# First block: the inner layer of the compressed keys and values with its operands exchanged, in four column tiles

## The reference

```python
def compress_blocks(tok, tok_idx, pos_emb, w1, w2):
    b, _, g, dh = tok.shape
    blk = tok[:, tok_idx] + pos_emb[None, None, :, None, :]
    flat = blk.transpose(0, 1, 3, 2, 4).reshape(b, tok_idx.shape[0], g, CMP_LEN * dh)
    return jax.nn.gelu(flat @ w1) @ w2
```

## Time and profile before

| | |
|---|---|
| three runs | 1532.93, 1535.36, 1536.45 us; median 1535.36 us |
| profiled execution, from its first to its last instruction | 1526.7 us (its time as a run is not given apart) |
| busy: TensorE / VectorE / ScalarE / GpSimd | 1497.1 / 1085.7 / 782.3 / 59.4 us |
| TensorE's granted clock | 9 tenths or more of full speed in all forty slices |
| DMA | 296.54 MB, mean 194 GB/s |

### The profile page before, as it was taken

How to read it: one execution, slowest core, us unless ns; L and a number is a source line. 1 busy time by engine, 2 the same in 40 slices (tenths; PEclk the granted TensorE clock), 3 DMA queues, 4 the chain that set the end, 5 groups by cost and what they waited for, 6 DMA issues and landing times.

```text
span 1526.7 us, 29330 instructions
## 1 busy us (share of the span) xinstructions
PE 1497.1 (98%) x12160; PEld 1457.3 (95%) x12160; DVE 1085.7 (71%) x1927; ACT 782.3 (51%) x1366; POOL 59.4 (4%) x61
## 2 busy tenths in 40 slices
PE   9999999999999999999999999999999999999999
PEld 8888899999898899999999989999999999999999
DVE  8777788887768778888984477665468646766653
ACT  6554586534644567633545545544444554454442
POOL 0000000000000000000030040000002102100000
PEclk9999999999999999999999999999999999999999
DMA  8124379997324269998343434545534444355552
GB/s 321 66 111 167 120 265 310 334 355 300 111 111 146 104 216 335 347 347 327 139 164 142 166 138 153 207 173 187 194 124 156 180 149 166 138 178 182 194 180 70
DMA packets 42435, 296.54 MB, mean 194 GB/s; under 512 B 5056, under 2 KB 5312, under 8 KB 6848
## 3 DMA queue, kind: packets, MB, share of 16 engines
q1 hardware_dynamic: 41888, 294.66, 52.7%
q10 hardware_dynamic: 416, 0.02, 0.0%
HBM read 293.61 MB, written 1.05 MB: 193 GB/s over the span
## 4 chain that ended last, share of the span: by engine, by line
PE 79%; DVE 10%; DMA 4%; ACT 3%; issue 2%; POOL 1%; SPq 0%; DVEq 0%; ACTq 0%
PE acc L766 23%; PE acc L767 23%; PE acc L768 23%; DMA ring<-stream 4%; DVE wL L1686 4%; ACT wH L1340 2%; PE ps_t L893 1%; PE acc L966 1%; PE acc L862 1%; PE ps_s L880 1%; PE ps_o L903 1%; PE ps_o L902 1%; PE ps_s L878 1%; PE acc L951 1%; PE acc L978 1%
## 5 line engine op out<-in xcount | busy, mean ns | idle before, releaser
L1686 DVE TENSOR_TENSOR wL<-ring,wH 128x1024 fp32r<-128x1024 f32 x444 | 548.6, 1243 | 274.6 <-ACT wH L1340 269.4
L766 PE MATMUL acc<-hH,wH 128*128 128x256 f32 x2208 | 638.4, 289 | 7.7 <-DVE wL L1686 3.5
L768 PE MATMUL acc<-hH,wL 128*128 128x256 f32 x2208 | 625.2, 283 | 0.0
L767 PE MATMUL acc<-hL,wH 128*128 128x256 f32 x2208 | 625.2, 283 | 0.0
L1340 ACT ACTIVATE wH<-ring 128x1024 fp32r<-128x1024 f32 x444 | 462.2, 1050 | 224.2 <-PE acc L768 117.5
L766 PEld LDWEIGHTS acc<-hH,wH 128*128 128x128 f32 x2208 | 423.8, 192 | 15.5 <-issue 9.6
L767 PEld LDWEIGHTS acc<-hL,wH 128*128 128x128 f32 x2208 | 424.0, 192 | 3.3 <-issue 2.6
L768 PEld LDWEIGHTS acc<-hH,wL 128*128 128x128 f32 x2208 | 423.8, 192 | 0.0
L766 PE MATMUL acc<-aH,wH 128*128 128x256 f32 x864 | 244.6, 283 | 0.8 <-DVE wL L1686 0.8
L767 PE MATMUL acc<-aL,wH 128*128 128x256 f32 x864 | 244.5, 283 | 0.0
L768 PE MATMUL acc<-aH,wL 128*128 128x256 f32 x864 | 244.5, 283 | 0.0
(11 more groups left out here) (321 smaller groups left out, 1803.4 us busy)
## 6 DMA issues: line engine op xcount, KB each, us to landing
ring<-stream SPq DMA_DIRECT2D x276, 1024.0 KB, 4.9
cst<-consts SPq DMA_DIRECT2D x1, 1347.0 KB, 16.0
x<-xin SPq DMA_DIRECT2D x4, 256.0 KB, 4.5
out<-x SPq DMA_DIRECT2D x4, 256.0 KB, 4.4
onc<-once SPq DMA_DIRECT2D x1, 516.0 KB, 16.3
v1all<-vec SPq DMA_DIRECT2D x1, 355.0 KB, 9.5
v2all<-vec SPq DMA_DIRECT2D x1, 330.0 KB, 17.5
nv<-pos SPq DMA_DIRECT2D x1, 256.0 KB, 4.5
```

Source lines behind the costliest of these rows:

```text
L766: pe.matmul(out, w[0], y[0], start=first, stop=False)
L767: pe.matmul(out, w[0], y[1], start=False, stop=False)
L768: return pe.matmul(out, w[1], y[0], start=False, stop=last)
L1686: TTN(wL[:, n % SPLIT, :], ring[:, g % RING, half * UNIT:(half + 1) * UNIT], wH[:, n % SPLIT, :].bitcast(F32), ALU.subtract).then_inc(lo_r ...
```

## The change

The two operands of the inner layer change places. The blocks, now padded to 32 columns (a memset writes the two spare ones), are the stationary operand, and the chunk's 128 columns of weights are moved. Chunk m goes to partitions 32 (m mod 4) to 32 (m mod 4) + 31 of the bank, so each quarter of the partitions sums four chunks. The products no longer take turns with a projection; they follow it as a group (`hidden_in_quarters`), before the scores. ScalarE copies the 128 x 128 result to `quarters`. A new product at the end of slots 6 and 7, `hsk` and `hsv`, takes the quarters as stationary operand and a constant 0/1 matrix `fold` as the moved one; it adds the quarters and turns the result back to 128 x 32. ScalarE copies 30 of these columns to `gel`.

```diff
-END1 = {5: ["hidk"], 6: ["mk0", "mk1", "mk2"], 7: ["hidv", "mk3", "mk4"], ...
+END1 = {5: ["hidk"], 6: ["mk0", "mk1", "mk2", "hsk"], 7: ["hidv", "mk3", "mk4", "hsv"], ...
...
+    put("fold", (i[:, None] % 32 == np.arange(32)[None, :]).astype(np.float32))
...
-        fk = [big[:, at:at + 2, :].rearrange("p a s -> p (a s)")[:, 0:480]
+        fk = [big[:, at:at + 2, :].rearrange("p a s -> p (a s)")
               .rearrange("p (m g n) -> p m g n", m=16, g=2) for at in (14, 6)]
+        quarters = [big[:, at, 0:P] for at in (14, 6)]
...
-                def project_among_hidden(name, kind, mid):
+                def hidden_in_quarters(kind):
 
                     j = ("k", "v").index(kind)
                     tl = tile("cmp" + kind, 0).rearrange("p (m n) -> p m n", m=16)
-
-                    def hidden(m):
-                        return pe.matmul(hid_acc[:, 0:30], tl[:, m, :], fk[j][:, m, :, :].rearrange("p g n -> p (g n)"),
-                                         start=m == 0, stop=m == 15)
-
-                    ... (24 products of the projection, one hidden product behind each from chunk 3 on)
+                    pe.wait_ge(f_ready, L * 2 + (j + 1))
+                    a = open_acc("hid" + kind)
+                    for m in range(16):
+                        at = 32 * (m % 4)
+                        last = pe.matmul(a[at:at + 32, 0:P], fk[j][:, m, :, :].rearrange("p g n -> p (g n)"), tl[:, m, :],
+                                         start=m < 4, stop=m >= 12)
                     last.then_inc(acc_full, 1)
-                    hidden(14)
-                    hidden(15).then_inc(acc_full, 1)
+
+                def hidden_summed(kind):
+
+                    drained("hid" + kind)
+                    a = open_acc("hs" + kind)
+                    pe.matmul(a[:, 0:32], quarters[("k", "v").index(kind)], C("fold"), start=True, stop=True)\
+                        .then_inc(acc_full, 1)
...
-                    elif END1.get(i, [""])[0][:3] == "hid":
-                        project_among_hidden(u, END1[i][0][3], lambda: middle(i))
                     else:
                         project(u, hs, mid=lambda: middle(i))
+                        if END1.get(i, [""])[0][:3] == "hid":
+                            hidden_in_quarters(END1[i][0][3])
...
                         if name[:3] == "hid":
-                            take(A1, name, L, gel[:, 0, 30 * (name == "hidv"):30 * (name == "hidv") + 30], n=30)
+                            take(A1, name, L, quarters[name == "hidv"], n=P)
+                        elif name[:2] == "hs":
+                            a = full(A1, name, L)
+                            act.activation(gel[:, 0, 30 * (name == "hsv"):30 * (name == "hsv") + 30]
+                                           .rearrange("p (g n) -> p g n", g=2),
+                                           a[:, 0:32].rearrange("p (g n) -> p g n", g=2)[:, :, 0:N_CMP], ACT.Copy)\
+                                .then_inc(acc_drained[A1.bank(name)], 1)
...
+                    nc.vector.memset(fk[j][:, :, :, N_CMP:NP16], 0.0)
                     for g in range(2):
-                        part = fk[j][:, :, g, :]
+                        part = fk[j][:, :, g, 0:N_CMP]
...
-                        dve.wait_ge(acc_drained[A1.bank("hid" + kind)], A1.drained("hid" + kind, L))
+                        dve.wait_ge(acc_drained[A1.bank("hs" + kind)], A1.drained("hs" + kind, L))
```

More of the change, by code:

```diff
@@ L194 @@
 ROPES1 = ["q0", "ks", "q1"] + [u for i in range(SLOTS1) for u in MID1.get(i, [])]
-END1 = {5: ["hidk"], 6: ["mk0", "mk1", "mk2"], 7: ["hidv", "mk3", "mk4"], 8: ["mv0", "mv1", "mq0"], 9: ["mq1", "mq2"],
+END1 = {5: ["hidk"], 6: ["mk0", "mk1", "mk2", "hsk"], 7: ["hidv", "mk3", "mk4", "hsv"], 8: ["mv0", "mv1", "mq0"], 9: ["mq1", "mq2"],
         10: ["kcc", "mq3", "mq4", "vbd"], 11: ["cs0", "cs1"], 12: ["rs0", "rs1"],
@@ L337 @@
                           ("mask", 384), ("cmask", 192), ("ckeep", 192), ("bmask", 6),
-                          ("decay", RET_HEADS * S), ("invc", 2 * S)])
+                          ("decay", RET_HEADS * S), ("invc", 2 * S), ("fold", 32)])
 VEC1, VEC2 = {}, {}
@@ L943, in _ @@
                 uq_of = lambda tl: tl[:, UQ:UQ + 960].rearrange("p (c n) -> p c n", c=2)
-                def project_among_hidden(name, kind, mid):
+                def hidden_in_quarters(kind):
                     j = ("k", "v").index(kind)
                     tl = tile("cmp" + kind, 0).rearrange("p (m n) -> p m n", m=16)
-                    def hidden(m):
-                        return pe.matmul(hid_acc[:, 0:30], tl[:, m, :], fk[j][:, m, :, :].rearrange("p g n -> p (g n)"),
-                                         start=m == 0, stop=m == 15)
[L954 to L969, removed]
-                    last.then_inc(acc_full, 1)
-                    hidden(14)
-                    hidden(15).then_inc(acc_full, 1)
+                    pe.wait_ge(f_ready, L * 2 + (j + 1))
[4 more added lines that the diff above has]
+                                         start=m < 4, stop=m >= 12)
+                    last.then_inc(acc_full, 1)
+                def hidden_summed(kind):
[3 more added lines that the diff above has]
+                        .then_inc(acc_full, 1)
                 def mla_queries(hh):
@@ L1106, in after @@
                                 retention_scores([n, n + 1] if n < 4 else [n])
+                        elif name[:2] == "hs":
+                            hidden_summed(name[2])
                         elif name != "cs1" and name[:3] != "hid":
```

## The result

| | before | after |
|---|---|---|
| median of six runs each, us | 1531.91 | 1524.30 |
| lowest to highest, us | 1527.02 to 1536.45 | 1520.21 to 1526.99 |
| span of the profiled execution, us | 1526.7 | 1519.7 |
| TensorE busy, us | 1497.1 | 1490.3 |

The ratio is 0.9947, with a 95% interval of 0.9929 to 0.9965: the change makes the kernel faster by half a per cent. The forecast was 1527.2 us, which is 0.9947 of the 1535.36 us that it started from. The size of the change came out and its level did not: 1524.3 is 2.9 us under the forecast, and 0.2 us under the low end of the range. That the two ratios agree to four digits is luck, since the interval of the measured one alone is 0.0036 wide.

The account below looks back on a forecast made before the run. TensorE was taken to bound the kernel, busy 1497.1 of 1526.7 us. Four times 3.46 us removed less 1.41 added saves 8.2, giving a span of 1518.5; with 8.7 up to the run median, 1527.2 us, range 1524.5 to 1533.

Parts of the forecast that it names:

- What bounds the kernel: Whole kernel: TensorE, busy 1497.1 of 1526.7 us, so a microsecond less on it should be a microsecond less of span.
- Removed, 3.46 us each: Slots 5 and 7 of both layers: the hidden products' cost, 6.84 less 3.38 us in each of four stretches, 13.8 us in all.
- Added, 1.41 us each: TensorE, each of four places: 0.30 us for tiling changes, 0.89 for the sixteen calls, 0.22 for the fold.
- complete overlap of four column tiles: New group of sixteen calls: 4 rounds of 2 records, 8 × 0.111 = 0.89 us, carried over from row-tiled pairs; chance 0.62.
- Rival 1: New group: strict order or slow sequencer halves the overlap; 2.4 us each, 4.3 saved in all, 1531.1 us; chance 0.20.
- the other form of the rival: New group: the sequencer can't feed four tiles; each load or product takes 28 ns, 64 × 0.028 = 1.8 us.
- Rivals 2 and 3: New group: column tiles don't overlap, 1537.8 us, chance 0.09; or each record pays load and stream in turn, 1552, chance 0.04.
- Rival 4: Changed stretches: the gain is there but waited away at a small margin or by VectorE, about 1535 us; chance 0.05.
- small margins: Bank turns at hsk and rqa, 0.1 to 0.5 us: costed at nothing; missed, some 0.1 to 0.3 us each.
- The 0.14 us between mk1's bank and the next projection: After hsk: mk1's bank is free at 82.76 while rqa, now waiting for it, opens at 82.9.
- What moves later: Transfers and later stages: the later stage starts earlier as a whole and gives nothing back; ring-slot margin 1.2 us.
- How the numbers follow: Final sum: span 1526.7 − 8.2 = 1518.5 us, plus some 8.7 from span to the shown runs' median, gives 1527.2.

## Why the change came out right and the level did not

**What bounds the kernel: right.** TensorE is busy for the whole of each changed slot, before and after, and each is shorter by what its own work lost. That the span lost 7.0 us where TensorE's busy time lost 6.8 agrees, but both hold the stretches that vary.

**Removed, 3.46 us each: right.** The slots fell from 6.84 to 4.49 us, and to 3.38 remain 1.10 for what was added there.

**Added, 1.41 us each: 1.34.** Overlap and changeovers were put at 1.19 and came to 1.10; the fold at 0.22 and came to 0.24. Four times 3.46 less 1.34 is 8.5 us, forecast 8.2; between the medians of the two kernels lie 7.6. The step that carried the most doubt, complete overlap of four column tiles read off two row tiles, held to the round.

**Rival 1, overlap by halves: wrong.** It needed a group of 1.8 to 1.9 us. A strict order of records would let a call's second record hold back the next call, so no more than two could run side by side; the group took 1.01 us, 3.6 times less than the 3.61 us of one tile. In the records the four tiles of a round start 7 ns apart (71.680, 71.686, 71.693, 71.700) and the next round 0.11 to 0.13 us later. The kernel with the paired keys' products shows whose records they are, because the second record of a call carries its signal: the first records of mk0 and mk1 start at 78.657 and 78.664, both second ones only at 78.924 and 78.930. So a call's second record doesn't hold back the next call in another tile. Nor does the other form of the rival hold, 28 ns for each load or product: with twice the products 128 of them take 1.88 us, 15 ns each. The Trainium skill (TensorE: Matmul & The Clock Gate, Part 3) states that matmuls start and end in strict program order. If the two records of a 32-bit product follow each other in the program, which the traces don't tell, these times do not agree with it. The same part gives 2.38 times for three column tiles of 512 columns; here three took 1.43 us against 3.61, 2.5 times with 16 calls that don't divide by three.

**Rivals 2 and 3, no overlap and loads in turn: wrong** in the kernel, and measured apart from it: with one tile the kernel is back at before's time, and a record costs 0.113 us, hardly more than its stream.

**Rival 4, a gain waited away: wrong** here, and right one step further on. None of the small margins was missed, so pricing them at nothing was right. The 0.14 us between mk1's bank and the next projection was real, though: once the keys' products were made 0.43 us shorter, the wait stood exactly there.

**What moves later: right.** SP issues its transfers 2.67 us earlier (72.82 against 75.49) and nothing collides with them. Nothing was said of the half clock behind the compressed scores or of the feed-forward stage of layer 1, and as the second profiles show, both vary by as much without the change.

**The step that failed** is the term of 8.7 us under "How the numbers follow", which takes the forecast span to a time: the level. It added to the forecast span 8.7 us, the distance between before's profiled execution and the median of the three runs shown, as if that were a fixed distance. It isn't: over six runs each, the median lies 5.2 us above the profiled span in the kernel before (1531.91 and 1526.7) and 4.6 in the changed one (1524.30 and 1519.7). The profiled execution of the changed kernel has a span of 1519.7 us and took 1521.52, and in every run on record, of every kernel here, a run is 1.75 to 1.88 us above its own span. So before's profiled execution was itself, by estimate, a run of 1526.7 + 1.8 = 1528.5 us, which lay 4 to 8 us below the three that were shown. That was to be read as a fourth sample: the kernel's executions spread over 1528 to 1537 at least, and a median of three from such a spread is uncertain by some 3 us, an estimate. The three happened to be high; why isn't shown. The median over six is 1531.91 us, 3.5 lower, and the sets measured beside the experiments, each on another chip, gave 1530.48, 1532.96 and 1532.83. From 1531.91 the same forecast ratio gives 1523.8, and 1524.3 was measured. The range's low end allowed the level 1 to 2 us, and was cut at 1524.5; 3 us of allowance would have held the time.

## What to carry to other kernels

Where a product moves 32 columns or fewer behind full loads and can be cut into independent sums, try four column tiles with a fold: here they took 1.34 us instead of 3.46. Price the group at the fullest tile's records times the time of one (0.111 us at 128 moved columns in 32 bit), plus a tenth of a microsecond, plus the fold. Before an engine is made faster ahead of a small rotation of buffers, work out for each buffer whose copy the next user waits for: an order with the short product first kept 0.2 us of a gain that the other order gave back, and moved the wait that was left to another product. And take the level of a forecast from all samples there are, the profiled execution among them, and give the range the spread that they show.

## What was not expected of the hardware

A busy TensorE can lose its clock. Sixteen products of 128 loaded and 30 moved columns in a row (3.5 to 4.0 us, no idle time) brought a granted clock of 0.50, 1.2 GHz, for several microseconds, from within the group or just behind it. It did so at seven of eight groups in two profiled executions, and by 99 us the kernel was about 6 us behind; by their mean clock, most of its other runs lost much less. The same sixteen woven among long products, as before had them, or cut into two groups of eight, kept 1.00; so did a group of the same length with 32 loaded and 128 moved columns. The stretches behind the compressed scores, products of 16 moved columns, cost 1.6 us in some executions and are absent in others. What in these groups brings the clock down wasn't separated further.
